# Latent norms, transposes and values of the attention made inside the input projection, with the token columns moved to its middle

## What is computed

```python
h = x * (1 + sc1) + sh1
cols = h @ p['w_in']
mla_cols, hg_cols, rw_cols = _split(cols, (MLA_COLS, HG_COLS, RW_COLS))
q_c, ckv, krope = _split(mla_cols, (MLA_Q_RANK, MLA_KV_RANK, MLA_ROPE))   # 384, 256, 32
ckv = _rmsnorm(ckv, p['mla_kv_norm'])
q = (_rmsnorm(q_c, p['mla_q_norm']) @ p['mla_w_uq'])...                    # 8 heads of 64 + 32
k_ckv = jnp.concatenate([ckv_c, ckv], axis=1)                              # grid tokens: 256 cached + 512
kv = (k_ckv @ p['mla_w_ukv'])...                                           # keys and values of 8 heads
mla_o = _mla_attend(q_nope, q_rope, k_nope, k_rope, v)
```

## Time and profile before

| | |
|---|---|
| median of 3 runs | 3517.41 us (3515.18 to 3517.89) |
| profiled execution | 3520.81 us |
| its span in the trace | 3519.0 us |
| TensorE busy, share of the span | 2804.8 us, 80% |
| VectorE, ScalarE, GpSimd busy | 38%, 15%, 20% |
| mean granted TensorE clock | 0.901 of full speed |
| projection, layer 1: first transpose to last matmul | 93.26 to 313.70 us |
| attention, layer 1: first matmul after the values (L706) | 345.79 us |
| the same two, layer 2 | 2031.07 and 2062.55 us |

### The profile page before, as it was taken

The page is one execution under the profiler, slowest core; times in us unless marked ns, Lnnn a source line. Parts: engine busy times, 40 slices in busy tenths (PEclk is TensorE's granted clock), DMA queues, the critical chain, the costliest instruction groups (busy, mean ns, idle before and its releaser), DMA issues. The chain is left out here.

```text
span 3519.0 us, 73007 instructions
## 1 busy us (share of the span) xinstructions
PE 2804.8 (80%) x32780; PEld 1886.2 (54%) x32780; DVE 1328.5 (38%) x2741; ACT 516.2 (15%) x987; POOL 692.8 (20%) x844
## 2 busy tenths in 40 slices
PE   5998885638584999999979978564776669999992
PEld 1555554538434666666435645453763456666661
DVE  1101668784624121111250046787654321111215
ACT  0102331131101000100110033302211100010001
POOL 0000908343120000000020054472411100000002
PEclk9999996769886999999989999776897789999996
DMA  8300000000052988898651000000005079898861
GB/s 344 128 19 35 1 9 3 7 1 3 3 215 84 390 336 332 333 346 345 249 244 54 1 35 1 9 3 7 3 2 199 29 273 346 341 351 341 336 245 63
DMA packets 68806, 533.90 MB, mean 152 GB/s; under 512 B 12656, under 2 KB 14512, under 8 KB 32144
## 3 DMA queue, kind: packets, MB, share of 16 engines
q1 hardware_dynamic: 65424, 518.75, 38.0%
q0 software_dynamic: 3072, 10.49, 1.1%
HBM read 520.43 MB, written 8.78 MB: 150 GB/s over the span
## 5 line engine op out<-in xcount | busy, mean ns | idle before, releaser
L2264 PEld LDWEIGHTS ps<-arena 128*64 128x64 f32 x16384 | 579.8, 138 | 102.4 <-issue 99.8
L2264 PE MATMUL ps<-arena 128*64 128x80 f32 x16384 | 600.8, 234 | 29.5 <-DVEq L2363 19.5
L2277 PE MATMUL ps<-arena 128*128 128x512 f32 (+1 forms) x1024 | 469.4, 602 | 5.2 <-ACT arena L2325 4.6
L2386 DVE TENSOR_TENSOR arena<-arena,ps 128x32 f32<-128x32 f32 (+1 forms) x192 | 45.1, 263 | 683.8 <-ACT arena L2333 683.8
L533 PE MATMUL ps<-arena 128*128 128x128 f32 (+1 forms) x1088 | 296.4, 435 | 5.3 <-DVE arena L586 5.3
L2277 PEld LDWEIGHTS ps<-arena 128*128 128x128 f32 (+1 forms) x1024 | 164.0, 169 | 219.8 <-issue 208.9
L2036 POOL DMA_INDIRECT arena<-h_d,arena x32 | 39.8, 1244 | 1015.5 <-DVEq L2357 910.7
L533 PEld LDWEIGHTS ps<-arena 128*128 128x128 f32 x1088 | 164.9, 192 | 137.0 <-issue 131.2
L2368 DVE TENSOR_TENSOR arena<-arena,ps 128x512 f32<-128x512 f32 x160 | 109.9, 687 | 271.1 <-PE ps L2291 214.9
L2333 ACT ACTIVATE arena<-ps 128x160 f32<-128x160 f32 x128 | 38.9, 304 | 942.7 <-PE ps L2264 942.7
L590 DVE COPY arena<-ps 128x128 f32<-128x128 f32 (+3 forms) x48 | 16.3, 340 | 399.4 <-PE ps L533 287.6
(11 more groups left out here) (331 smaller groups left out, 4071.9 us busy)
## 6 DMA issues: line engine op xcount, KB each, us to landing
arena<-in_ex_w SPq DMA_DIRECT2D x128, 2048.0 KB, 8.5
arena<-in_ex_w SPq DMA_DIRECT2D x128, 1024.0 KB, 7.7
arena<-in_ada_w SPq DMA_DIRECT2D x24, 2048.0 KB, 15.4
arena<-in_w_t SPq DMA_DIRECT2D x34, 512.0 KB, 3.4
arena<-in_w_out SPq DMA_DIRECT2D x4, 2048.0 KB, 10.4
arena<-in_w_tok SPq DMA_DIRECT2D x2, 3712.0 KB, 16.9
h_d<-x_sb SPq DMA_DIRECT2D x10, 512.0 KB, 2.6
arena<-mod_d SPq DMA_DIRECT2D x8, 512.0 KB, 6.6
```

What stands on the lines that cost most here:

```text
L2264: m = nc.tensor.matmul(gated(j)[c * 64:(c + 1) * 64, f, a, :], w13[:, j, a, k, f * P + c * 64:f * P + (c + 1) * 64], xT[:, x % 2, k, :], s ...
L2277: m = nc.tensor.matmul(ps[0:CAP if x % 2 == 0 else P, 4 + h, :], rows[x % 2][:, f, :], w2[:, (f // 2 + 2) % 4, f % 2, h * 512:(h + 1) * 51 ...
L2386: m = nc.vector.tensor_tensor(rows[b][:, 2 * j:2 * j + 2, to:to + c1 - c0], hs[:, j % 2, :, c0:c1], gated(j)[:, :, 1, c0:c1], ALU.mult)
```

## The change

The work on the latents leaves `phase_attention` and becomes groups of `phase_project`. The order of the groups there is now: ten x groups, column blocks 0 to 5, all 15 tok groups, blocks 6 to 10, five "cq" groups (the query transposes of one tile each), block 11, seven "ckv" groups (the key transposes), blocks 12 and 13, seven "V" groups, blocks 14 to 16. The norms stand on ACT after the last tok group has been copied out and before ACT's next group, and on DVE before its second group behind the tok groups. The copies out of PSUM go by the number of the group, even to ACT and odd to DVE, whatever the kind. SP loads the attention weights once the tok groups are done, behind the load of block 11 (they lie in the memory that `w_tok` has left), and stores `n_ckv` and `n_kr` behind the last column block's load. The arena grows from 40600 to 41800 words per partition, since ring and attention memory now live at the same time. Attention's DVE no longer waits for its stores, nor its PE for the copies of `V`.

```diff
+    tokw, _ = e.part(e.FREE, KD, TOKC)
+    mem, z = attention_memory(e)
+    st, z = e.part(z, 2 * TILES)
     ring, z = e.part(z, WRING, KD, P)
...
-    groups += [("T", c, g) for c in range(NT) for g in (1, 0)]
-    groups += [("tok", t, s) for t in range(TILES) for s in range(3)]
+    columns = [[("T", c, 1), ("T", c, 0)] for c in range(NT)]
+    after = {5: [("tok", t, s) for t in range(TILES) for s in range(3)], 10: [("cq", t, 0) for t in range(TILES)],
+             11: [("ckv", t, 0) for t in range(KT)], 13: [("V", t, 0) for t in range(KT)]}
...
-                    sp.wait_ge(S["pj_ps"], NX + 2 * (c - WRING + 1))
+                    sp.wait_ge(S["pj_ps"], column_end(c - WRING))
                 sp.dma_start(ring[:, c % WRING], d["w_t"][l, c]).then_inc(S[f"ld_wt{c % WRING}"], 16)
                 if c == WRING - 1:
                     sp.dma_start(tokw, d["w_tok"][l]).then_inc(S["ld_tokw"], 16)
+                if c == 2 * WRING - 1:
+                    sp.wait_ge(S["pj_ps"], TOKENS)
+                    for dst, src in ((uq, d["w_uq"][l]), (uk, d["w_uk"][l]), (uv, d["w_uv"][l]),
...
+                elif kind == "cq":
+                    pe.wait_ge(S["q_norm"], a + 1)
+                    for k in range(3):
+                        i = nc.tensor.transpose(ps[:, n % 8, k * P:(k + 1) * P], tok[:, a, k * P:(k + 1) * P], e.ident[:, :])
+                elif kind == "ckv":
+                    if a < TILES:
+                        pe.wait_ge(S["kv_norm"], a + 1)
...
+                elif kind == "V":
+                    pe.wait_ge(S["ld_mla"], 80)
+                    pe.wait_ge(S["pj_act"], (GROUPED[2] + 1) // 2)
+                    pe.wait_ge(S["pj_dve"], GROUPED[2] // 2)
+                    for k in range(2):
+                        i = nc.tensor.matmul(ps[:, n % 8, :], ckvT[:, k, a * P:(a + 1) * P], uv[:, k, :], start=k == 0, stop=k == 1)
...
             for n in range(0, len(groups), 2):
+                if n in (TOKENS, TOKENS + 1):
+                    act.wait_ge(S["pj_act"], (TOKENS + 1) // 2)
+                    act.wait_ge(S["pj_dve"], TOKENS // 2)
+                    for t in range(TILES):
+                        a_.add(nc.scalar.activation(V[:, 0, 0:QR], tok[:, t, 0:QR], ACT.Square, accum_out=st[:, t:t + 1]))
...
             for n in range(1, len(groups), 2):
+                if n in (TOKENS + 2, TOKENS + 3):
+                    dve.wait_ge(S["rms"], 1)
+                    v.link(nc.vector.reciprocal(st[:, :], st[:, :]))
...
 def phase_attention(e):
...
-            for t in range(TILES):
-                pe.wait_ge(S["q_norm"], t + 1)
...
-            pe.wait_ge(S["tk_ev"], KT)
-            pe.wait_ge(S["tq_ev"], TILES)
-            for t in range(KT):
-                if t >= 4:
-                    pe.wait_ge(S["v_ev"], t - 3)
...
-                elif i == 0:
-                    pe.wait_ge(S["v_ev"], KT)
...
-            v.join()
             v.link(nc.vector.tensor_tensor(rt[:, 0:NSM], Kh[NOPE:QK, 0, g0:], e.rope[NOPE:QK, 0, :], ALU.mult))
...
-            dve.wait_ge(S["st_cache"], 32)
```

## The result

The changed kernel takes **3488.84 us** (median of 4 runs, 3484.37 to 3492.05) against 3517.65 us of the kernel before (4 runs, 3515.18 to 3521.21): a ratio of 0.9916 with a 95% interval of 0.9899 to 0.9934, 0.84% faster. The forecast was 3488.0. In five more runs on another occasion it took 3487.46 (ratio 0.9915, 0.9902 to 0.9929).

A forecast was written before the change was run, and what follows sets the result against it. No engine bounds the whole; between projection and rotation TensorE lost time waiting and at half clock. Replacing 32.09 and 31.48 us by 17.1 per layer saves 29.4: 3517.41 - 29.4 = 3488.0 us, range 3482 to 3498.

The forecast's parts named there:

- The four terms: What replaces the stretch from the projection's last matmul to the keys' rotation: 17.1 us per layer in sum.
- Transposes: In the projection: 5 query and 7 key tiles, three transposes each, at full clock, 4.0 us per layer.
- values: In the projection: seven tiles of two 512-wide matmuls at full clock, 12.0 us per layer.
- The wait: Ahead of the first V group, for ACT's copy of block 13's group: 0.4 us, bounds 0.1 and 1.0.
- the start: Attention's start behind the projection's last matmul, formerly hidden under idling: 0.7 us, ends 0.6 and 1.5.
- the two ends: Alternative sizes per layer: 8.3 us for transposes at the lower clock, 13.85 for values with a slow start.
- What was taken at nothing: Norms, copies, loads, stores and rotation cost nothing; norms have 32 us of slack behind five column blocks.
- A: Rival: the clock falls in the projection's transposes; +8.0 us per layer, 3504 us; chance 0.05.
- B: Rival: attention starts late, its code fetched without cover; up to 3494 us, likelier 3491; chance 0.10.
- D: Rival: clock stays low through following column blocks, slower than before; 3540 us with three blocks per layer; chance 0.02.
- E: Rival: norms or loads come late inside the projection and TensorE waits there; 3512 to 3520 us; chance 0.03.
- C: Rival: attention's low clock moves, up to 3.2 us either way per layer; counted inside the forecast's 0.80.

The follow-up runs named there:

- run without cover: Changed kernel with the query groups directly behind the tok groups, no column blocks between: 3512.82 us, ratio 0.9983 to the kernel before.
- the relaxed wait: Changed kernel, but the first V group waits only for the key groups' copies, not block 13's: 3489.72 us.
- one block: Changed kernel with one column block instead of five between tok groups and query groups: 3490.07 us.
- the first set: First four experiments, sharing a chip: changed kernel again, V group's wait narrowed, values back in attention, only norms and loads moved; kernel before took 3517.44 us there.

## Why the prediction was right

**The four terms.** Transposes 3.9 us against 4.0, values 12.1 against 12.0, the wait 0.57 against 0.4, the start 0.66 against 0.7. Sum 17.26 against 17.1. Each was taken from the row nearest in condition (same shape, full clock), not from the average of the old stretch, and the runs bear that choice out: the two ends that I kept for transposes and values at half clock did not occur in either profile of the changed kernel.

**The wait** is ScalarE's 0.28 us copy, with 0.03 us ahead of it (289.66 to 289.69) and 0.26 behind it. The last part I had at 0.06; it is the only term sized clearly wrong, by 0.2 us. The variant without the wait confirms its cause.

**What was taken at nothing** cost nothing: no gap at the transposes, at block 12 or at the last block, and no copy late. The cover was five blocks where one is enough, and where it is gone the 8.3 us are back.

**The rivals.** A (the clock falls in the transposes) fell with a clock of 1.00 there, and for good with 13.1 us of transposes. B (late code): the start is 0.66 us, so neither a fetch nor a longer block end shows. The Trainium skill (Runtime: NRT & Kernel Launch, Instruction fetch mechanics) lets one expect a stall at a taken branch whose target is not at hand; no run here shows one at this place. D and E did not happen; the run without cover is E made real, and even it is not slower than before.

**C, the clock in attention**, did happen, in both directions. From the rotation to HGRN's first multiply the changed kernel took 172.1 and 175.3 us in its first profile and 172.1 twice in the second. The difference is the clock in head 0; layer 2 of the first profile, then of the second:

```profile
2045.00:2054.00 9.00, 9.00 (x57) 5.24 (x58) 4.56 (x8) 2.34 (x5) 8.74 (x8) 0.81 0.00 0
```

```profile
2045.00:2054.00 9.00, 9.00 (x66) 5.30 (x64) 5.78 (x12) 3.33 (x7) 8.74 (x8) 1.00 0.00 0
```

Times there are 172.1 to 172.3, about 173.7, or 175.3 to 175.5: no fall, a short one, or a longer one. The kernel before had the long one in 5 of its 6 stretches. The changed kernel and its three variants that leave at least the transposes in the projection and have full cover (the relaxed wait, the values back, one block) had it in 1 of 10, and the middle one in 1. That is a gain of about 2 us per layer that my sum did not have. Against it, in these profiles the scans take on average 1.2 us longer per layer than in the three of before, and the way from the experts' first matmul to the second layer's projection takes 2.5 us longer, that from layer 2's experts to the program's end 0.7. The forecast's exactness of one microsecond is thus partly luck: the stretch is explained to 0.3 us, and beside it stand shifts of several us with both signs.

Whether the fall in head 0 hangs on what stands ahead of attention or is chance stays open; no run here was made to tell. The other runs give a hint. The kernel before with useless matmuls moves nothing and only keeps TensorE busy, and it has 172.2 and 173.9 us, not once the long time. The eightfold transposes have 173.7 twice, the run without cover 175.3 and 172.1, the norms alone 172.1 and 175.4.

**Where the 29 us come from**, by the stretches in the profiles: norms and loads under cover 17.7 (8.4 + 9.4), transposes with their copies and the clock that came with them 12.3, values -1.0. In one layer the kernel before's stretch differs by up to 0.5 us between executions, so each of the first two is good to about 1 us at best. The medians of the first set divide the gain less sharply: 15.7 us for norms and loads, 14.6 for the transposes, and 0.3 against the values' move, with single runs of the norms-only kernel 9 us apart.

## What to carry to other kernels

Moving work of the busy engine to another dense place gave nothing here; what gave was to put the other engines' short chains, and the copies out of PSUM that TensorE then waited for, behind work that is dense anyway. Measure the chain and give it one piece of work longer than it: here 8.65 us for 8.3. Before moving the large part, try the small ones alone: norms and transposes without the values reached the same time.

## What the runs showed of the hardware

Float32 transposes in a row hold the full clock for 13.1 us (granted 1.00, 0.109 us each). A block's end costs TensorE 0.65 us from its last matmul to the next block's first, with a 0.29 us copy on VectorE in between (the changed kernel). With a 0.28 us copy on ScalarE there it is 0.62 (values back, norms only), and with ScalarE's 256-wide copy of 0.38 us it is 0.73 (the kernel before with useless matmuls); I had allowed up to 1.5. And in sparse stretches, head 0 of attention and the delta-rule scan, the granted clock falls in some executions of a program and not in others, which moves a layer by some 3 us each time (172.1 or 175.4 us in attention, about 452 or 455.5 in the scans). A difference of that size between two single profiles shows nothing.
